# Four steps of modulation on matmuls of 32 columns, loads issued ahead of two stages, and eight sinks to an instruction

## The reference

```python
mod = silu(c) @ w_ada + b_ada                      # one row of 6 * 1024
sh1, sc1, gt1, sh2, sc2, gt2 = split(mod, 6)
h = rms_norm(x, g_pre_mix) * (1 + sc1) + sh1
qa, ka, va, cq, ckv, kidx, widx = split(h @ w_in)  # 1220 columns
# A: 8 heads, 64-token chunks that see their own and the previous chunk, with a sink per head:
m = max(max(logits, -1), sink); p = exp(logits - m)
out_a = (p / (sum(p) + exp(sink - m))) @ v
# B: 8 heads; an indexer scores all visible keys, each query keeps its 256 best, softmax over those
mix = concat(out_a, out_b) @ w_o
x = x + gt1 * rms_norm(mix, g_post_mix)
h2 = rms_norm(x, g_pre_ffn) * (1 + sc2) + sh2
gate, up = split(h2 @ w_gate_up)                   # 2 * 2816 columns
x = x + gt2 * rms_norm((silu(gate) * up) @ w_down, g_post_ffn)
```

## Time and profile before

| | us |
|---|---|
| median of 3 runs (lowest, highest) | 3321.71 (3314.52, 3324.0) |
| profiled execution | 3318.27, span 3316.5 |
| TensorE busy / weight loads | 2950.7 (89%) / 2411.2 (73%) |
| VectorE, ScalarE, GpSimd busy | 1688.8 (51%), 1573.0 (47%), 313.5 (9%) |
| `mixing`, `project_output`, `ffn` | about 42 to 1590, 1590 to 1804, 1804 to 3316 |

### The profile page before, as it was taken

The page is one execution under the profiler, slowest core; times in us unless marked ns, Lnnn a source line. Parts: engine busy times, 40 slices in busy tenths (PEclk is TensorE's granted clock), DMA queues, the critical chain, the costliest instruction groups (busy, mean ns, idle before and its releaser), DMA issues. The chain is left out here.

```text
span 3316.5 us, 42857 instructions
## 1 busy us (share of the span) xinstructions
PE 2950.7 (89%) x14649; PEld 2411.2 (73%) x14649; DVE 1688.8 (51%) x3080; ACT 1573.0 (47%) x3023; POOL 313.5 (9%) x990
## 2 busy tenths in 40 slices
PE   6678888787888888899896999999999999999997
PEld 2466666666676667788785887888878887888876
DVE  2246768686878867844454343244423443254422
ACT  0457787877787776875333222232223222232222
POOL 0012222212121210110011000000000000000000
PEclk8788888888998888789998999999999999999999
DMA  5000000000000000110555333343333432343323
GB/s 213 11 25 24 25 20 29 15 19 17 20 20 11 20 6 28 45 55 11 194 177 157 96 95 95 114 146 95 97 119 109 128 98 90 120 143 97 95 89 108
DMA packets 316074, 254.86 MB, mean 77 GB/s; under 512 B 9152, under 2 KB 271904, under 8 KB 315808
## 3 DMA queue, kind: packets, MB, share of 16 engines
q1 hardware_dynamic: 282544, 236.29, 22.9%
q10 hardware_dynamic: 33392, 16.81, 1.8%
HBM read 219.50 MB, written 33.57 MB: 76 GB/s over the span
## 5 line engine op out<-in xcount | busy, mean ns | idle before, releaser
L1962 ACT ACTIVATE p_hi<-raw 128x1024 fp32r<-128x1024 f32 x264 | 279.3, 1058 | 694.7 <-PE dbank L1933 355.7
L2036 DVE TENSOR_TENSOR p_lo<-raw,p_hi 128x1024 fp32r<-128x1024 f32 x264 | 323.4, 1225 | 426.6 <-ACT p_hi L1962 426.4
L1133 ACT ACTIVATE signs<-score,pick 128x512 int8<-128x512 f32 (+6 forms) x224 | 304.3, 1358 | 29.1 <-POOL pick L629 20.3
L1286 DVE TENSOR_SCALAR_CACHE_REDUCE above<-score,cand 128x384 uint8<-128x384 f32 (+6 forms) x224 | 315.8, 1410 | 4.3
L1111 ACT ACTIVATE logit<-tbank 128x512 f32<-128x512 f32 (+3 forms) x448 | 214.7, 487 | 207.5 <-PE tbank L847 203.8
L863 PE MATMUL obank<-vb,logit 128*128 128x64 f32 x2176 | 304.8, 286 | 0.0
L1914 PE MATMUL gbank<-x_hi,p_hi 128*128 128x512 f32 x704 | 275.5, 391 | 29.2 <-DVE p_lo L2036 29.2
L863 PEld LDWEIGHTS obank<-vb,logit 128*128 128x128 f32 x2176 | 298.8, 211 | 0.0
L1931 PE MATMUL dbank<-p_hi,a_hi 128*128 128x512 f32 x704 | 278.8, 396 | 17.0 <-DVE a_lo L2064 14.0
L847 PE MATMUL tbank<-ident,logit 128*128 128x128 f32 x1336 | 250.7, 301 | 42.9 <-ACT logit L1101 41.5
L729 PE MATMUL work<-w_in,h_T 128*128 128x512 f32 (+1 forms) x768 | 281.8, 514 | 0.7 <-ACT h_T L927 0.7
(11 more groups left out here) (219 smaller groups left out, 5240.2 us busy)
## 6 DMA issues: line engine op xcount, KB each, us to landing
raw<-in_w_gate_up SPq DMA_DIRECT2D x176, 512.0 KB, 3.8
raw<-in_w_down SPq DMA_DIRECT2D x88, 512.0 KB, 3.7
ada<-in_w_ada ACTq DMA_DIRECT2D x32, 512.0 KB, 3.8
wada<-in_w_ada SPq DMA_DIRECT2D x4, 2048.0 KB, 15.5
x_in<-in_x SPq DMA_DIRECT2D x16, 512.0 KB, 3.9
mixT<-oT SPq DMA_DIRECT2D x32, 256.0 KB, 2.3
mix<-mixT SPq DMA_DIRECT2D x16, 512.0 KB, 6.2
x_rows<-in_x SPq DMA_DIRECT2D x16, 512.0 KB, 4.6
```

The source lines that it names most:

```text
L1133: nc.scalar.activation(signs[:, 0:L], score[:, b % 2, 0:L], ACT.Sign, scale=-1.0, bias=pick[:].bitcast(F32), accum_out=less_more[:]).then_ ...
L1286: link(nc.vector.tensor_scalar(above[:, 0:L], score[:, b % 2, 0:L], cand[:].bitcast(F32), None, ALU.is_ge, ALU.add, accum_out=count[:]), b ...
L1962: nc.scalar.activation(p_hi[:, s], raw[:, s], ACT.Copy).then_inc(panel_high, 1)
L2036: nc.vector.tensor_tensor(p_lo[:, s], raw[:, s], p_hi[:, s].bitcast(F32), ALU.subtract).then_inc(panel_ready, 1)
```

## The change

Three things are changed at once.

1. **The four rows of modulation** are made in four steps, one for each row, at h = 1 and h = 5 of the "B" heads of b = 13 and b = 14. The operands change places: `c_act`, one column broadcast to 32, is stationary, and w_ada streams past it, 256 columns at a time, in four parts that write four different quarters of the partitions. A load brings 1024 columns (4 MB in pieces of 4 KB) into the space of `w_in`, which is free after the last projection. The rows lie ready for GpSimd without a turn, and go to DRAM during b = 15.
2. **Loads ahead of two stages.** `Kept` and `OutputWeights` hold buffers across stages. w_o and the first tile of the mixed tokens are loaded during b = 15 (`first_loads`), the first x of `ffn`, its first two panels and the row gt2 ahead of the last two tiles of `project_output`. In `ffn` x is split in four parts, and the first product waits for them two k at a time.
3. **Sinks.** `negmax` keeps the eight heads of a block apart, GpSimd adds the sinks to them in one instruction of eight columns (`shift_sinks`), and ScalarE takes the eight exponentials in one (`exponent_of_sinks`), three heads after the block's last.

```diff
@@ mixing_steps
-            if (h == 5 and b < NB - 4) or (h % 2 and b == NB - 4) or b in (NB - 3, NB - 2):
-                modulate()
-            if b == NB - 1 and h == 0:
-                add(("mod_rows",))
+            if b in (NB - 3, NB - 2) and h in (1, 5):
+                add(("mod", 2 * (b - NB + 3) + h // 4))
@@ mixing, TensorE
-                for k in range(KD):
-                    mm = nc.tensor.matmul(ps[:, 0:1], ada[:, k, :], shared.c_act[:, k:k + 1],
-                                          start=(k == 0), stop=(k == KD - 1))
+                each = P // MOD_PARTS
+                for k in range(KD):
+                    for j in range(MOD_PARTS):
+                        mm = nc.tensor.matmul(ps[j * each:(j + 1) * each, 0:MOD_COLS],
+                                              shared.c_act[:, k:k + 1].to_broadcast([P, each]),
+                                              ada[:, k, j * MOD_COLS:(j + 1) * MOD_COLS],
+                                              start=(k == 0), stop=(k == KD - 1))
@@ mixing, SyncE, after the store of block ("B", NB - 2)
+                    first_loads()
...
+                    sp.wait_ge(mod_made, 3)
+                    for j in range(MOD_PARTS):
+                        sp.dma_start(w["mods"].rearrange("r (j n) -> j r n", n=MOD_COLS)[j:j + 1],
+                                     mod_rows[row_of(j)]).then_inc(mod_stored, 16)
...
+                    sp.dma_start(shared.later.mix0, w["mixT"].rearrange("(k p) t -> p k t", p=P)[:, :, 0:P]
+                                 ).then_inc(shared.later.mix0_in, 16)
@@ mixing, ScalarE
-                if kind == "A":
-                    nc.scalar.activation(exp_sink[:, o % 2, h:h + 1], sink[:, h:h + 1], ACT.Exp,
-                                         bias=negmax[:, i % 4:i % 4 + 1])
...
+                act.wait_ge(sink_shifted, b + 1)
+                nc.scalar.activation(exp_sink[:, o % 2, :], sink_less[:], ACT.Exp).then_inc(sink_done, 1)
@@ mixing, GpSimd
+                nc.gpsimd.tensor_tensor(sink_less[:], sink[:], negmax[:, o % 2, :], ALU.add).then_inc(sink_shifted, 1)
@@ mixing, VectorE
                 if kind == "A":
+                    dve.wait_ge(sink_done, b + 1)
                     link(nc.vector.tensor_tensor(sums, sums, exp_sink[:, o % 2, :], ALU.add))
@@ project_output, SyncE, ahead of the last two tiles
+            sp.dma_start(ahead.x_lo[:].bitcast(F32), h2T_dram[:, :, 0:TOK]).then_inc(ahead.x_loaded, 16)
+            for s in range(2):
+                sp.dma_start(ahead.raw[:, s].rearrange("p (k n) -> p k n", n=P),
+                             w["w_gate_up"].rearrange("(k p) n -> p k n", p=P)[:, :, s * D_FF:s * D_FF + P]
+                             ).then_inc(ahead.raw_in[s], 16)
+            sp.dma_start(ahead.row[:], w["mods"][GT2:GT2 + 1, :].partition_broadcast(P)).then_inc(ahead.row_in, 16)
@@ ffn, TensorE
+                    if begins and k % 2 == 0:
+                        pe.wait_ge(x_split, 4 * c + k // 2 + 1)
@@ ffn, ScalarE
-            x_high_part(0)
-            for s in range(2):
-                panel_high_part(0, 0, s)
+            for part in range(4):
+                x_high_part(0, part)
+                if part < 2:
+                    panel_high_part(0, 0, part)
```

More of the change, by code:

```diff
@@ L484, in mixing @@
         oT = sb("oT", [P, 4, P])
[L485 to L489, removed]
+        ada = shared.later.w_o
+        mod_rows = x_in[:].rearrange("p (r n) -> p r n", n=MOD_COLS)
+        mod_bias = pj[:, 0:D].rearrange("p (r n) -> p r n", n=MOD_COLS)
+        mod_gain = shared.later.rest[:, 0:D].rearrange("p (r n) -> p r n", n=MOD_COLS)
         squares = h_T[:].rearrange("p k t -> p (k t)")
@@ L669, in _ @@
                     shift()
-                if s[0:4] == ("head", "B", NB - 1, 4):
+                    if heads:
+                        shift_sinks(heads - 1)
+                    heads += 1
+                if s[0:4] == ("head", "B", NB - 1, 0):
                     modulate()
@@ L1456, with project_output @@
 OUT_ORDER = [("A", 0), ("A", 1)] + [o for b in range(NB) for o in (("A", b + 2), ("B", b)) if o[1] < NB]
-AFFINE_LOADS = 2 + sum(g is not None for g in MOD_GAINS)
+AFFINE_LOADS = MOD_PARTS * (1 + sum(g is not None for g in MOD_GAINS))
 N_CONST = 9
-def project_output(nc, w):
+def project_output(nc, w, later, ahead):
     with ExitStack() as ctx:
@@ L1475, in sem @@
             return ctx.enter_context(nc.semaphore(name))
-        wo = sb("wo", [P, KD, D])
+        wo, wo_in = later.w_o, later.wo_in
         wo_hi = sb("wo_hi", [P, KD, D], F32R)
@@ L1498, in project_output @@
         rows_in = sem("rows_in")
-        wo_in = [sem("wo_in%d" % k) for k in range(KD)]
         wo_high = sem("wo_high")
@@ L1714, in tile @@
                 nc.vector.tensor_tensor(h2[:, s], h2[:, s], rows[:, 2, :], ALU.add).then_inc(h2_made, 1)
-            low(0, 0)
+            low(0, 0, later.mix0)
             for k in range(KD):
@@ L1728, in _, with ffn @@
                 tile(NB // 2 - 1, s, s == 0)
-def ffn(nc, w):
+def ffn(nc, w, ahead):
     HALF = D // 2
@@ L1905, in _, with up_product @@
         def _(pe):
-            def up_product(c, j, s, which):
+            def up_product(c, j, s, which, begins=False):
                 n = 2 * j + which
@@ L1936, in chunk @@
             def chunk(c, first, last):
-                with pe.Fori(0, KF // 2) as jj:
-                    pe.wait_ge(x_split, 2 * (c + 1))
+                for s in range(2):
+                    for which in range(2):
+                        up_product(c, s, s, which, begins=(s == 0 and which == 0))
+                with pe.Fori(1, KF // 2) as jj:
                     for s in range(2):
@@ L2096, in chunk @@
                 if not last:
-                    x_low_part(c + 1)
+                    for part in range(4):
+                        x_low_part(c + 1, part)
                 for s in range(2):
@@ L2105, in _ @@
             nc.vector.sem_inc(act_ready, 2)
-            x_low_part(0)
-            for s in range(2):
-                low_part(s, s)
+            for part in range(4):
+                x_low_part(0, part)
+                if part < 2:
+                    low_part(part, part)
             dve.wait_ge(row_in, 16)
@@ L2137 @@
     w["x1"] = nc.dram_tensor("x1", (T, D), F32).ap()
-    with ExitStack() as ctx:
-        shared = Resident(ctx, nc)
-        modulation(nc, w, shared)
-        mixing(nc, w, shared)
-    project_output(nc, w)
-    ffn(nc, w)
+    with ExitStack() as kept_ctx:
+        kept = Kept(kept_ctx, nc)
+        with ExitStack() as later_ctx:
+            later = OutputWeights(later_ctx, nc, kept)
+            with ExitStack() as ctx:
+                shared = Resident(ctx, nc, kept, later)
+                modulation(nc, w, shared)
+                mixing(nc, w, shared)
+            project_output(nc, w, later, kept)
+        ffn(nc, w, kept)
     r = _run(nc, [arrays], core_ids=[0])
```

218 lines of the change are left out of this document (123 added, 95 removed).

## The result

The changed kernel took 3283.35 us (median of four runs, 3276.38 to 3285.69) against 3318.11 for the kernel before: a ratio of 0.9893, 95% interval 0.9873 to 0.9913. Forecast were 3274 and a range of 3257 to 3307.

A forecast was written before the change was run, and what follows sets the result against it. TensorE was taken to bound "A" heads and "B" heads of b = 13 and 14, nobody alone b = 12. Terms summed to -45.6 from the profiled 3318.3, so 3272.7, raised to 3274 for the median; range 3257 to 3307.

The forecast's parts named there:

- Sign: Whole kernel: the changed kernel is faster than the one before, chance 0.87.
- Seams, -19.0: Starts of output projection and ffn: first products come sooner with loads made ahead, gaining 5.5 and 13.5 us.
- Steps of b = 13 and 14, "all 33": Old modulation steps in b = 13 and 14: TensorE bounds there, so removing 17.9 and 15.1 us gains all 33.
- New steps, +28.4: Four added modulation steps in b = 13 and 14: passes half overlapped, 7.1 us each, chance 0.42.
- the rival at 3.6 us a step: New steps: all four parts run side by side, 14 us for four steps, total 3263; chance 0.18.
- The trade in that stretch: b = 13 and 14: old steps -33 and slow stretches -5 against new steps +28.4.
- b = 12, -8: Old steps in b = 12: 12.5 us of TensorE removed where it is busy four fifths of the time, taken 8.
- b = 0 to 11, -5: Old steps in b = 0 to 11: 24.5 us removed, mostly swallowed by TensorE's waits for VectorE, taken 5.
- Sinks, -4: Sinks in mixing: 0.29 us saved at each of 14 waits of TensorE for exponentials in "A" heads, 4 us.
- Slow stretches, -5: b = 13 and 14: about seven stretches at 1.2 GHz behind old steps vanish, 0.8 us each, 5 us.
- nothing but the seams: Rival: removed steps of b = 0 to 12 and sinks gain nothing, new steps cost what old did; -19, about 3300; chance 0.07.

The follow-up runs named there:

- e5: Changed kernel with the loads of w_o, the first tile and ffn's first operands issued at the start of their own stages again; 3302.09 us, ratio 0.9951.
- e1: Kernel before with the 32 old product steps of modulation cut to one of eight matmuls each; 3293.67 us, ratio 0.9930.
- e4: Changed kernel with ScalarE's 32 sums of signs for block 15 taken over 1024 of 2048 scores; 3271.53 us, ratio 0.9857.
- e2: Changed kernel with the two loops of a product step exchanged, so each quarter's eight passes stand together; 3311.52 us, ratio 0.9980.
- e3: Changed kernel with each of the four new product steps cut to the first of its eight parts; 3278.97 us, ratio 0.9882.
- e6: Changed kernel with a sink's exponential taken per head again, without GpSimd's sums; 3277.32 us, ratio 0.9878.
- e11: e7 with a sink's exponential taken per head again, as in e6; 3263.62 us, ratio 0.9828.
- e7: Changed kernel with second and fourth product steps moved behind the queries of B blocks 14 and 15, third to head 4 of block 14; 3263.02 us, ratio 0.9836.
- e10: e7 with the two product steps behind the queries cut to one of eight parts; 3274.15 us, ratio 0.9864.
- e12: e11 with block 15's sums of signs spread over one head more of block 14, VectorE's closing actions in the last two heads; 3267.81 us, ratio 0.9846.

## Why the prediction was right, and where it was not

Sign, range and the outer mechanism held; several terms were wrong in size. The old steps of b = 13 and 14 were booked some 24 us too high and the new ones some 20 too high. That these two nearly cancel is luck: without the second error the time would lie some 29 us above the forecast instead of 9.

- **Seams, -19.0.** The first `pbank` product came 3.9 us sooner behind B15's mark, the first `gbank` product another 14.8 sooner: -18.7, and both at the forecast distance from their blocks. Right. The whole part behind the mark is 20.6 shorter than before, 14.8 shorter than in e5; by medians e5 gives 19 to 21.
- **Steps of b = 13 and 14, "all 33".** This is the step that failed. By e1 they were worth about 9 (7.6 for seven eighths). The prediction read 70.9 of 77.7 and 75.8 of 80.0 as "TensorE bounds"; it meant only that nobody else was further behind, and part of those 70.9 us was work at the lower clock (0.76 on the mean). ScalarE, at 63.1 in b = 13, had a chain with GpSimd in it whose waits do not show as busy time, and halving its search for block 15 was worth 10 us (e4).
- **New steps, +28.4.** Busy time 18.1, as fully side by side as the rival at 3.6 us a step had it; the prediction's reason for half ("only the second pass of one part and the first of the next can overlap") is refuted by e2 and the 3.66 us. What they cost in time is another matter: 3.9 for seven eighths (e3), plus about 4 for the places in which they stand (e3 against e1), together about 8.
- **The trade in that stretch.** -33 - 5 + 28.4 should have given -9.6; the two blocks gave -1.5 (163.9 to 162.5 us between marks), and with A block 15's heads ahead of them nothing. The prediction's warning was that ScalarE's wait inside a step would make TensorE wait for exponentials later in b = 13. It did not come true: ScalarE's one long wait, 6.20 us, stands in b = 14, and TensorE's waits for exponentials (L1101, now L1153) were 6.8 us before and 6.6 after.
- **b = 12, -8.** Measured -10.4 between the marks of B11 and B12, and -11.7 in e1. Right in kind, a little low: it is nearly the full 12.5 us of the steps, though TensorE was less busy there (63.6 of 80.7) than in b = 13 and 14. The busy share put the two places in the wrong order.
- **b = 0 to 11, -5.** Measured -2.6, in a stretch where one program varies by 8 us: not decided.
- **Sinks, -4.** No gain seen: without the new form the median was 3.7 us lower in e6 and 0.6 higher in e11, both within the spread. ScalarE's busy time in `mixing` fell by 23 us (1084.3 to 1060.9) without the time following.
- **Slow stretches, -5.** From B12's mark to B14's the mean granted clock was 0.84 before, 0.86 after and 0.86 in e1: little was gained, and the old steps were not the main cause. Slow stretches are seen behind waits of TensorE, at the queries and at the 2.87 us above, and not where these are filled (e7, e10).

The Trainium skill's figure in "TensorE: Matmul & The Clock Gate", Part 3, 2.38 times for three parts of 32 columns, points the right way, and the trace goes on from it: four parts gave 11.50 / 3.66 = 3.14 times here.

The rival "nothing but the seams" had the right balance for b = 13 and 14 (the new steps cost there what the old ones did) and the right word for the sinks. It was wrong for b = 12.

What stays open: whether the move of the third step alone would bring the 5.6 us; how the 10 us of e4 divide between ScalarE's shorter work and GpSimd's earlier thresholds; and what makes one program reach B12's mark at 1312 in one execution and at 1320 in another.

## What to carry to other kernels

A busy share of 0.91 to 0.95 is no bound as long as the second engine stands at 0.7 to 0.8 with waits in its chain: cut a part of the work and look (e1) before booking its full length as gain. The place of a piece of work can be worth more than its size: three steps moved to where TensorE or the engine ahead of it had to wait anyway brought 13.7 us, taking nearly all of the four away brought 3.9. And compare profiles by marks inside the program: a stretch that begins at the first difference was steady to 1 us where whole executions were 9 apart.

## What the runs showed of the hardware

Four float32 matmuls of 32 columns each, on different quarters of the output's partitions, ran at the same time when they stood next to each other: 64 passes of 256 columns in 3.66 us, against 11.50 with the quarters one after the other. Behind a wait of TensorE of 4.5 to 7.6 us at the queries the granted clock was 0.50 to 0.66 over the next 5 us; behind one of 2.87 us in the changed kernel it was 0.50. Where the wait was only 0.95 us (block 15 in e7, e11 and e12) or 2.00 us (block 14 in e12) it was 1.00.
